# Eight-head layer's front: gate and value units a channel block ahead, position columns, taps on ScalarE

## The reference, cut to what matters

```python
h = rms_norm_2(x, norm1_g)
proj = h @ w_in      # q 512 | k_c v_c k_s v_s k_w v_w, 128 each | g_nsa 24 | u_conv 1024 | g_merge 2048
y_attn = nsa_attention(q, ..., g_nsa, ...) @ w_attn_br
y_conv = conformer_conv(u_conv, ...) @ w_conv_br
x = x + (g_a * y_attn + g_b * y_conv) @ w_out          # g_a, g_b = sigmoid(g_merge)

def compress(kv, pe, w1, w2):     # 31 blocks of 32 tokens, stride 16; for keys and for values
    blk = kv[:, idx] + pe         # pe: 32 position vectors of 64
    return gelu(blk.reshape(..., 32 * 64) @ w1) @ w2

def conformer_conv(u, dw_w, dw_b, ln_g, ln_b, w_proj):
    a, gate = split(u)            # 512 channels each
    z = a * sigmoid(gate)
    z = causal_dwconv(z, dw_w) + dw_b          # 31 taps for each channel
    return silu(layer_norm(z, ln_g, ln_b)) @ w_proj
```

## Time and profile before

| | |
|---|---|
| median of 3 runs | 1985.27 us (1985.1 to 1985.39) |
| profiled execution, its own time | 1981.76 us |
| its span | 1980.0 us |
| mean granted clock of TensorE | 0.991 |
| TensorE busy | 1938.3 us, 98% |
| VectorE / ScalarE / GpSimd busy | 958.4 / 722.6 / 732.4 us |
| `round_unit` on ScalarE, `wlo` on GpSimd | 1060 ns and 2403 ns, mean of one |

### The profile page before, as it was taken

How to read it: one execution, slowest core, us unless ns; L and a number is a source line. 1 busy time by engine, 2 the same in 40 slices (tenths; PEclk the granted TensorE clock), 3 DMA queues, 4 the chain that set the end, 5 groups by cost and what they waited for, 6 DMA issues and landing times.

```text
span 1980.0 us, 22714 instructions
## 1 busy us (share of the span) xinstructions
PE 1938.3 (98%) x9094; PEld 1565.8 (79%) x9094; DVE 958.4 (48%) x1649; ACT 722.6 (36%) x1172; POOL 732.4 (37%) x309
## 2 busy tenths in 40 slices
PE   8999999999998999999999999899999999999998
PEld 7777888888886777888888888788677888888887
DVE  7563564441036445264444005894665765555202
ACT  6554422222244444332222224223654343333221
POOL 2333244444441222524444452342112444444442
PEclk9999999999999999999999999999899999999999
DMA  4412122332231222312233231321111222322222
GB/s 161 167 60 79 55 95 98 99 101 96 96 107 54 86 95 75 117 44 96 99 99 100 97 107 65 127 96 55 42 33 54 96 86 97 100 100 97 96 96 86
DMA packets 52152, 178.60 MB, mean 90 GB/s; under 512 B 5680, under 2 KB 5824, under 8 KB 51792
## 3 DMA queue, kind: packets, MB, share of 16 engines
q1 hardware_dynamic: 45776, 164.09, 25.1%
q10 hardware_dynamic: 6272, 13.07, 1.9%
HBM read 175.00 MB, written 6.33 MB: 92 GB/s over the span
## 4 chain that ended last, share of the span: by engine, by line
PE 87%; DVE 6%; ACT 3%; issue 2%; DMA 1%; POOL 1%; SPq 0%; DVEq 0%; ACTq 0%
PE bank L401 24%; PE bank L403 24%; PE bank L402 24%; PE bank L1384 2%; PE bank L1369 1%; PE bank L1137 1%; PE bank L1131 1%; PE bank L1132 1%; PE bank L1770 1%; PE bank L843 1%; PE bank L1347 1%; DVE tmp L1049 1%; PE bank L1040 1%; POOL wlo L385 1%; DMA raw<-stream 1%
## 5 line engine op out<-in xcount | busy, mean ns | idle before, releaser
L385 POOL TENSOR_TENSOR wlo<-raw,whi 128x1024 fp32r<-128x1024 f32 x285 | 684.6, 2403 | 1203.5 <-ACT whi L380 1203.4
L380 ACT ACTIVATE whi<-raw 128x1024 fp32r<-128x1024 f32 x287 | 304.1, 1060 | 851.6 <-PE bank L403 828.2
L401 PE MATMUL bank<-hh,whi 128*128 128x512 f32 x1384 | 545.1, 394 | 7.6 <-POOL wlo L385 6.3
L402 PE MATMUL bank<-hl,whi 128*128 128x512 f32 x1384 | 540.8, 391 | 0.0
L403 PE MATMUL bank<-hh,wlo 128*128 128x512 f32 x1384 | 540.7, 391 | 0.0
L401 PEld LDWEIGHTS bank<-hh,whi 128*128 128x128 f32 x1384 | 261.6, 189 | 71.4 <-issue 14.5
L403 PEld LDWEIGHTS bank<-hh,wlo 128*128 128x128 f32 x1384 | 261.1, 189 | 55.3
L402 PEld LDWEIGHTS bank<-hl,whi 128*128 128x128 f32 x1384 | 261.5, 189 | 53.2 <-issue 0.2
L514 DVE TENSOR_TENSOR tmp<-bank,rs 128x512 f32<-128x512 f32 x154 | 105.3, 689 | 237.8 <-PE bank L403 223.5
L401 PE MATMUL bank<-fh,whi 128*128 128x512 f32 x496 | 192.9, 389 | 0.0
L402 PE MATMUL bank<-fl,whi 128*128 128x512 f32 x496 | 192.9, 389 | 0.0
(11 more groups left out here) (281 smaller groups left out, 2424.8 us busy)
## 6 DMA issues: line engine op xcount, KB each, us to landing
raw<-stream SPq DMA_DIRECT2D x307, 512.0 KB, 3.4
bias_scratch<-rel_scratch ACTq DMA_DIRECT2D x1, 4096.0 KB, 18.9
biasB<-bias_scratch ACTq DMA_DIRECT2D x16, 256.0 KB, 2.8
w<-w_in ACTq DMA_DIRECT2D x2, 1024.0 KB, 5.9
out<-y ACTq DMA_DIRECT2D x8, 256.0 KB, 2.1
x<-x_in SPq DMA_DIRECT2D x3, 512.0 KB, 8.9
x<-x_in SPq DMA_DIRECT2D x2, 256.0 KB, 5.5
cst<-consts_in SPq DMA_DIRECT2D x1, 448.0 KB, 4.3
```

The costliest lines, as they stand in the source:

```text
L380: e.activation(slot[u][0][:, :], raw[u % 2][:, :], ACT.Copy).then_inc(*w_hi.done(u))
L385: e.tensor_tensor(slot[u][1][:, :], raw[u % 2][:, :], slot[u][0][:, :].bitcast(F32), ALU.subtract)\
L401: e.matmul(o, wh, h, start=first, stop=False)
L402: e.matmul(o, wh, l, start=False, stop=False)
```

## The change

In the front TensorE takes za and zg of a block earlier and fewer gates between them: `GATES_AFTER` gives gates 0, 1 | 2 | 3 to 5 | 6 to 11 after the four blocks. VectorE scales za and zg of block c+1 inside the taps of block c (`CONV_BESIDE`, by block and tap), with two pairs of PSUM banks for the sums. Taps 0 and 1 of each block are ScalarE's. The sums of the conv result come ahead of kd0, those of the squares right behind it; qC0 comes last. The position vectors are two more columns of `kp`, so the 16 one-column matmuls of each compression are gone; `kp` is laid out by token modulo 16. The compressions have banks 2 and 3, and run behind one another. kd1 becomes a unit of turn 0, beside vC1. The low parts of the conv branch go from VectorE to GpSimd, behind unit 217.

```diff
...
+GATES_AFTER = ((0, 1), (2,), (3, 4, 5), (6, 7, 8, 9, 10, 11))
...
-    kp = [sb(f"kp{j}", [P, 2, T], R4 + 4 * KB * j) for j in range(2)]
+    kp = [sb(f"kp{j}", [P, 2, 8, 34], R4 + 4 * KB * j) for j in range(2)]
...
+            if u == FIRST["C"] + 27:
+                for c in range(4):
+                    e.wait_ge(*high.at(("z", c)))
+                    e.tensor_tensor(ol[:, 4 + c, :], zc[:, c, :], oh[:, 4 + c, :].bitcast(F32), ALU.subtract).then_inc(*z_low.done(c))
...
-        for c in range(4):
+        for c, gates in enumerate(GATES_AFTER):
             if c:
                 e.wait_ge(*evicted.at(("za", c - 1)))
                 project(e, 0, hh, hl, ("za", c))
                 e.wait_ge(*evicted.at(("zg", c - 1)))
                 project(e, 1, hh, hl, ("zg", c))
...
+            if c == 1:
+                e.wait_ge(*evicted.at("g"))
+                for t in range(QT):
+                    mm = e.transpose(bank[5][:, t * P:(t + 1) * P], tmp[7][:, t * P:(t + 1) * P], ident)
+                mm.then_inc(*turned.done("g"))
+            for j in gates:
+                if j:
+                    if j >= 2:
+                        e.wait_ge(*evicted.at(("gate", j - 2)))
+                    project(e, 2 + j % 2, hh, hl, ("gate", j), between={1: lambda: spread_tokens_pe(e, 6, "j3", 16)} if j == 1 else {})
         for s in range(2):
             e.wait_ge(*evicted.at((("za", "zg")[s], 3)))
             project(e, s, hh, hl, ("cmp", s))
-        project(e, 4, hh, hl, ("kd", 0))
         e.wait_ge(*formed.at(("conv", 3)))
         for c in range(4):
             pe_sum(e, 7, zc[:, c, :], c == 0, c == 3, ("zc", c))
...
+        project(e, 4, hh, hl, ("kd", 0))
         for c in range(4):
             e.wait_ge(*squared.at(("zc", c)))
             pe_sum(e, 7, tmp[c % 2][:, :], c == 0, c == 3, ("zc2", c))
+        project(e, 5, hh, hl, ("vC", 0))
+        e.wait_ge(*evicted.at(("gate", 11)))
+        compress_pe(e, 0)
         compress_pe(e, 1)
-        e.wait_ge(*evicted.at(("cmp", 0)))
-        project(e, 0, hh, hl, ("kd", 1))
         e.wait_ge(*evicted.at(("vC", 0)))
-        c_values_pe(e, 0, 1)
+        c_values_pe(e, 0, 0)
+        project(e, 1, hh, hl, ("qC", 0))
         e.wait_ge(*made.at(("hid", 1)))
-        e.matmul(bank[2][:, 0:2 * N_CMP], gg("w2k", 0, P), hid[0][:, 0:2 * N_CMP], start=True, stop=True)\
-            .then_inc(*mixed.done("kc"))
-        e.wait_ge(*evicted.at(("kc", 1)))
+        e.wait_ge(*stats.at((("zc2", 3), "mean")))
+        e.matmul(bank[7][:, 0:2 * N_CMP], gg("w2k", 0, P), hid[0][:, 0:2 * N_CMP], start=True, stop=True)
         for g in range(2):
             for h in range(2):
-                mm = e.matmul(bank[2][32 * h:32 * h + N_CMP, 64 * g:64 * g + 64],
+                mm = e.matmul(bank[7][32 * h:32 * h + N_CMP, 64 + 64 * g:128 + 64 * g],
                               hid[1][:, g * N_CMP:(g + 1) * N_CMP], gg("w2v", 0, 64), start=True, stop=True)
-        mm.then_inc(*mixed.done("vc"))
+        mm.then_inc(*mixed.done("kc"))
...
-        for n in range(16):
-            mm = e.matmul(bank[2][:, 64:65], w1[s][:, n, :], gg(name, n), start=n == 0, stop=n == 15)
+            at = (0, 0) if n < 8 else (1, 2)
+            mm = e.matmul(sums[:, :, at[0]:at[0] + 32], w1[s][:, n, :], kp[s][:, :, n % 8, at[1]:at[1] + 32],
+                          start=n == 0, stop=n == 15, skip_group_check=True)
         mm.then_inc(*mixed.done(("cmp", s)))
...
+    def compress_positions_dve(e, s):
+        for col, n in ((0, 0), (33, 8)):
+            e.tensor_copy(kp[s][:, :, :, col], gg(("pek", "pev")[s], n, 8).unsqueeze(1).to_broadcast([P, 2, 8]))\
+                .then_inc(*formed.done(("kp", s, n)))
...
+        conv_sigmoid_act(e, 0)
+        gate_act(e, 0)
+        conv_first_taps_act(e, 0)
+        gate_act(e, 1)
+        round_unit(e)
+        round_unit(e)
+        conv_sigmoid_act(e, 1)
         e.wait_ge(*turned.at("g"))
         e.activation(gtok[:, :, :], bank[5][:, :].rearrange("p (k c) -> p k c", c=P)[:, :, 0:24], ACT.Sigmoid)\
             .then_inc(*made.done("gtok"))
+        conv_first_taps_act(e, 1)
+        round_unit(e)
+        gate_act(e, 2)
+        round_unit(e)
+        round_unit(e)
+        conv_sigmoid_act(e, 2)
+        round_unit(e)
+        conv_first_taps_act(e, 2)
+        for j in (3, 4, 5):
+            gate_act(e, j)
+            round_unit(e)
+        round_unit(e)
+        conv_sigmoid_act(e, 3)
+        round_unit(e)
+        conv_first_taps_act(e, 3)
+        for j in range(6, 12):
+            gate_act(e, j)
+            if j < 11:
+                round_unit(e)
...
-                e.activation(kp[s][0:64, g, :], tmp[5 + s][r, :], ACT.Copy).then_inc(*made.done(("kp", s, 2 * g)))
-                e.activation(kp[s][64:128, g, 0:T - 1], tmp[5 + s][r, 1:T], ACT.Copy).then_inc(*made.done(("kp", s, 2 * g + 1)))
+                tokens = tmp[5 + s][r, :].rearrange("p (j r o) -> p o r j", r=8, o=2)
+                for o in range(2):
+                    e.activation(kp[s][64 * o:64 * o + 64, g, :, 1:33], tokens[:, o, :, :], ACT.Copy).then_inc(*made.done(("kp", s, 2 * g + o)))
...
-                branch_act(e, 0)
-                compress_act(e, 0)
-        round_unit(e)
+        branch_act(e, 0)
         act_root(e, rs[2], ("zc2", 3))
         round_unit(e)
+        for c in range(4):
+            e.wait_ge(*formed.at(("unit", c)))
+            e.activation(zc[:, c, :], zc[:, c, :], ACT.Silu, scale=gg("lng", c), bias=gg("lnb", c)).then_inc(*made.done(("z", c)))
+            e.wait_ge(*made.at(("z", c)))
+            e.activation(oh[:, 4 + c, :], zc[:, c, :], ACT.Copy).then_inc(*high.done(("z", c)))
+        compress_act(e, 0)
         compress_act(e, 1)
...
+        c_values_act(e, 0, 0)
...
+    def conv_first_taps_act(e, c):
+
+        e.wait_ge(*formed.at(("z", c)))
+        if c >= 2:
+            e.wait_ge(*formed.at(("conv", c - 2)))
+        if c == 1:
+            e.wait_ge(*made.at("gtok"))
+        zp, into = zpad[c % 2], CONV_BANKS[c % 2]
+        e.activation(into[0][:, :], zp[:, 0:T], ACT.Identity, scale=gg("dw", c * TAPS), bias=gg("dwb", c)).then_inc(*made.done(("tap", c, 0)))
+        e.activation(into[1][:, :], zp[:, 1:1 + T], ACT.Copy, scale=gg("dw", c * TAPS + 1)).then_inc(*made.done(("tap", c, 1)))
...
+    CONV_BANKS = ((bank[6], bank[7]), (bank[4], bank[5]))
+    CONV_BESIDE = {
+        (0, 4): ("gate", 1), (0, 19): ("in", 1), (0, 23): ("product", 1), (0, 28): ("gate", 2),
+        (1, 9): ("in", 2), (1, 13): ("product", 2), (1, 18): ("gate", 3), (1, 26): ("gate", 4),
+        (2, 3): ("gate", 5), (2, 17): ("in", 3), (2, 21): ("product", 3), (2, 26): ("gate", 6),
+        (3, 3): ("gate", 7), (3, 8): ("gate", 8), (3, 15): ("gate", 9), (3, 23): ("gate", 10)}
...
+        conv_in_dve(e, 0)
+        gate_dve(e, 0, 2)
+        conv_product_dve(e, 0)
         for c in range(4):
...
+            zp, into = zpad[c % 2], CONV_BANKS[c % 2]
+            for tap in range(2, TAPS):
+                if (c, tap) in CONV_BESIDE:
+                    what, j = CONV_BESIDE[c, tap]
+                    if what == "in":
+                        conv_in_dve(e, j)
+                    elif what == "product":
+                        conv_product_dve(e, j)
+                    else:
+                        gate_dve(e, j, 2 + j % 2)
+                s = into[tap % 2][:, :]
+                e.wait_ge(*(made if tap < 4 else formed).at(("tap", c, tap - 2)))
+                e.scalar_tensor_tensor(tmp[4][:, :] if tap == TAPS - 1 else s, zp[:, tap:tap + T],
+                                       gg("dw", c * TAPS + tap), s, ALU.mult, ALU.add).then_inc(*formed.done(("tap", c, tap)))
             e.wait_ge(*formed.at(("tap", c, TAPS - 1)))
-            e.tensor_tensor(zc[:, c, :], tmp[4][:, :], bank[7][:, :], ALU.add).then_inc(*formed.done(("conv", c)))
+            e.tensor_tensor(zc[:, c, :], tmp[4][:, :], into[1][:, :], ALU.add).then_inc(*formed.done(("conv", c)))
+        gate_dve(e, 11, 3)
         e.wait_ge(*formed.at(("conv", 3)))
+        for s in range(2):
+            compress_positions_dve(e, s)
...
         dve_mean(e, rs[2], 7, CONV_C, ("zc2", 3))
         dve_inverse(e, rs[2], ("zc2", 3))
         e.wait_ge(*stats.at((("zc2", 3), "inv")))
         for c in range(4):
             e.tensor_tensor(zc[:, c, :], zc[:, c, :], rs[2][:, :], ALU.mult).then_inc(*formed.done(("unit", c)))
+        e.wait_ge(*proj.at(("vC", 0)))
+        e.wait_ge(*made.at(("kp", 1, 3)))
+        dve_scale(e, 5, rs[0], tmp[6][:, :], ("vC", 0))
+        compress_dve(e, 0)
         compress_dve(e, 1)
...
         for g in range(2):
             e.memset(vcb[g][:, :], 0.0).then_inc(*formed.done(("zero_v", g)))
         e.memset(pC[:, :, :], 0.0).then_inc(*formed.done("zero_p"))
         e.memset(kcz[:, :, :, :], 0.0).then_inc(*formed.done("zero_k"))
+        c_bias_dve(e, 0)
+        e.wait_ge(*proj.at(("qC", 0)))
+        dve_scale(e, 1, rs[0], qC[0][:, :], ("qC", 0))
...
```

(65 more changed lines are left out.)

89 lines of the change are left out of this document (32 added, 57 removed).

## The result

The changed kernel takes 2004.89 us (median of 5 runs, 2002.01 to 2007.64) where the kernel before takes 1985.1 (5 runs beside it, 1982.75 to 1985.39): ratio 1.0104, 95% interval 1.0091 to 1.0118. It is slower by 20, and the forecast of 1969.9 was wrong. The profiled execution took 2002.01, its span is 2000.0.

The account below looks back on a forecast made before the run. TensorE, busy 98% of the span, was taken as the bound. Front 1.6 won and stretch behind the convolution 13.8 won sum to 15.4: 1985.27 - 15.4 = 1969.9 us, range 1965.5 to 1975.

Parts of the forecast that it names:

- kd1 itself is moved, not added: Turn 0: unit kd1 costs nothing extra there; only its late copies, 0.9 before the scores of turn 1, were charged.
- No queue of SP is passed: Unit loading behind the convolution: costed at nothing, since a unit loads once its low part two back is done.
- Rival 6: No change, 1985: TensorE held elsewhere by what it gains, as in front of gate 8; chance 0.02.
- Rival 5: Slower, about 1993: each block's rounding waits behind ScalarE's taps, four waits of 7.3 for one, 22 more; chance 0.04.
- The waits of the new front: TensorE's forecast idle times: 0.9 at za2, 3.5 at zg2, 3.5 plus 0.4 at the second sums, 0.9 at turn 1.
- The clock terms: Lower-clock costs: 1.3 behind the zg2 wait, 1.2 behind the wait at the second sums, 0.5 in the back-to-back compressions.
- rival 2: The clock falls neither at the two new waits nor in the compressions: 3.0 less, 1966.9; chance 0.12.
- the slow scores and the slow unit of turn 0: Turn 0: scores 2.2 and unit 0.9 too slow, put down to slow clock behind the one-column matmuls.
- The sum of 20.3: Gain behind the convolution before new costs: one-column matmuls 9.65, slow clock 7.15, two waits for VectorE 3.5.
- The eight taps on VectorE were therefore never worth anything by themselves: Convolution front: removing eight taps from VectorE only keeps it ahead, ending near 1337, 6 before TensorE comes.
- The one-column matmuls: Ahead of the compressions: removal from TensorE's chain wins 5.29 and 4.36, together 9.65, plus 7.15 of slow clock behind them.
- the fourth rival: GpSimd's low parts hold VectorE's normalising in turn 0: 1.6 over the spare 1.9, about 1 of clock, 1972.5; chance 0.05.

Follow-up runs that it names:

- e1: The changed kernel with one more round_unit on ScalarE at the end of turn 0; 1969.57 us, 0.9932 of the kernel before.
- e2: The kernel before with the last round_unit of its front taken away, nothing else; 2017.59 us, ratio 1.0169.
- e8: The changed kernel with the extra round_unit at the end of turn 6 in place of turn 0; 1971.67 us, 0.9926 of the kernel before.
- e3: e1 with VectorE taking the mean and centring the conv result before it scales kd0; 1964.17 us, 0.9903 of the kernel before.
- e10: e1 with the four low parts of the conv branch on VectorE again, not GpSimd; 1970.59 us, 0.9936 of the kernel before.
- e7: e1 with taps 0 and 1 of each block on VectorE again; 1976.55 us, 0.9952 of the kernel before.
- e6: e1 with 16 one-column matmuls put back ahead of each compression, their result unread; 1991.32 us, 1.0027 of the kernel before.

## Why the prediction was wrong

**The step that failed** is the one of turn 0, "kd1 itself is moved, not added". The only queue that the prediction checked for the move was SP's ("No queue of SP is passed"). I costed kd1's matmuls and copies, but each unit also has a call of `round_unit`, and the diff takes one out of the front and puts none into the turn. I walked the roundings of the new front one after another and never set their number beside the old one; the walk stopped at the scores of turn 1, and all that follows was carried over unchanged. It measured +34.4 (6.8 + 8.5 + 1.7 + 17.4). e1 takes 35 away with one call, e2 puts 34 on the old kernel by removing one (2017.59 - 1984.02), and e8, which makes the call up only at the end of turn 6, still wins nearly all of it back.

**Rival 6**, no gain because TensorE is held elsewhere, was the nearest in kind. I gave it 0.02 since it "would need 15 of waits that I found nowhere"; I had looked only up to turn 1. **Rival 5**, the other one with a late rounding, had the wrong place: the taps of ScalarE cost one wait of 3.03, not four of 7.3. Its "20 more than my front" does not follow from its own terms either (four waits of 7.3 against 7.3 - 1.6 are 23.5); its sum of about 1993 is made with the 22 and stands.

**The waits of the new front** were right. At za2 0.60 (0.9 forecast), at zg2 3.03 (3.5), at the second sums 3.61 (3.5; of the 0.4 that I added for a rounding between the squares there is little, the sums take 4.05, before 3.78), at turn 1 1.05 (0.9). e3 shows that the order of VectorE makes the 3.61, as argued.

**The clock terms** (1.3, 1.2 and 0.5) did not occur in the profiled execution of the changed kernel. Busy time by stretch, the share before the last two is PEclk:

```profile
1239.70:1400.00 160.30, 152.53 (x718) 123.12 (x716) 124.28 (x218) 68.50 (x102) 59.29 (x27) 1.00 0.26 89
```

So in this execution rival 2 came true for the front: it promised 3.0 more, and the front beat the forecast by 2.5. That was luck. In the executions of e1, e8 and e10, which have the same two waits, the clock fell behind the wait at zg2 in all three (0.91 in 1260 to 1280 in e1, 0.83 in 1270 to 1280 in e8 and e10), and behind the second one in two (0.66 and 0.71 in 1360 to 1370 in e8 and e10). Their fronts are 164.1, 166.7 and 166.8 long, the one of the changed kernel 162.5, and the forecast, 180.4 - 15.4, is 165.0: the terms of the two waits, 2.5 together, were sized about right. The third term, 0.5, has no counterpart: the two compressions behind one another ran at full pace, their 64 records in 7.1, and the scores of turn 0 record 2.43, as forecast.

**Where the clock fell before** was read wrong in one place. The prediction puts the slow scores and the slow unit of turn 0, 2.2 and 0.9, down to the one-column matmuls. But in the kernel before 1.00 is granted in 1393 to 1399, between the second row of them and those scores, and 0.50 in 1399.7 to 1406, at the two waits for VectorE of the earlier trace rows. The sum of 20.3 holds all the same, since the change takes both away.

**"The eight taps on VectorE were therefore never worth anything by themselves"** is wrong. With them on VectorE again the kernel is 5.5 to 7 slower (e7), with a wait of 3.60 at gate 8, where I had found 1.0 to spare: the six taps ahead of the scaling that it waits for are 4.0 (0.66 each) and use that up. The spare time there existed because ScalarE has them.

**The one-column matmuls** were put at 9.65 and the slow clock behind them at 7.15, 16.8 together; put back, they cost 18.5 in the profiled execution (e6). The order of size is right. That run has them ahead of each compression and not behind it, so it is not the same arrangement as in the old kernel.

**Low parts on GpSimd.** Four take 5.06, 1.27 each (1.2 forecast), and the fourth rival did not show: e10 has the same time.

**Left open.** What the move of kd1 into turn 0 and the layout of `kp` are worth by themselves was not tried. Why the clock falls behind a wait in one execution and not in another stays open.

## What to carry to other kernels

Where the order of a prefetch is written out by hand, count its calls up to every point that the change touches, in old and new, before costing anything: a pipeline that lost one place runs on without an error and pays wherever the prefetch stands behind work that waits. In the profile one reads it from what ends the idle time ahead of the prefetching op: if that was the consumer (as early as it can be) and is now a producer ahead of it in the same queue, the lead is gone. And walk a change to the end of the program, not to the end of the changed lines.

## What the runs showed of the hardware

The lower clock comes at different places from one execution to the next, in code that is the same: in the two executions above the slow stretches ahead of the front lie at 580 to 590 and 620 to 630 in the one, at 580 to 590, 620 to 640, 840 to 850 and 1210 to 1220 in the other. It goes with the spread of a kernel's runs: the fastest run of e1 (1967.26) has a mean granted clock of 0.993, the slowest (1973.14) 0.990, and 0.003 of 1970 is, as an estimate, 5.9: the whole difference. In e6 it is 0.988 at 1986.92 and 0.983 at 1994.82.

Matmuls that hold TensorE busy without a gap can still bring the clock down. In e6 TensorE is busy for all of 1376 to 1400, with no wait; 1.00 is granted in 1376 to 1380, and 0.50 in 1386 to 1400. The kernel before has the same: 0.50 in 1366 to 1372, with TensorE busy all the while. At the low level the 32 records of one column take as long as the 32 of 64 columns (6.93 and 7.07 us in e6), and at the full one 3.63 against half of 7.25 in e1. The Trainium skill (TensorE: Matmul & The Clock Gate, section HAM oscillation) speaks of gaps in which TensorE stands idle. Here the clock fell without one, and behind such gaps it did not always fall: behind the same wait of 3.61 it stayed at 1.00 in the changed kernel and in e1, and went to 0.50 in e6.
